# Moving VectorE's division and store of an attention head behind the second maxima of the next heads

## The reference

```python
def softmax_attend(q, k, v):
    s = jnp.einsum('bkgqd,bksd->bkgqs', q, k).astype(F32) * HEAD_DIM ** -0.5
    p = jax.nn.softmax(s, axis=-1).astype(v.dtype)
    return jnp.einsum('bkgqs,bksd->bkgqd', p, v)
```

## Time and profile before

| | |
|---|---|
| median of 3 executions | 6648.83 us (6646.48 to 6653.36) |
| the profiled execution | 6653.24 us |
| its span in the trace | 6651.5 us |
| TensorE busy | 4964.1 us, 75% of the span |
| VectorE busy | 2852.6 us, 43% |
| ScalarE busy | 1478.4 us, 22% |
| mean granted TensorE clock | 0.838 of full speed |

### The profile page before, as it was taken

One profiled execution on the slowest core, in us unless ns is written; L12 is line 12 of the kernel. 1 busy time (PEld: TensorE's weight loads), 2 busy tenths in 40 slices (PEclk: granted clock), 3 DMA queues, 4 the chain that ended last, 5 costly groups with the idle time before them and its releaser, 6 DMA issues. The chain is left out here.

```text
span 6651.5 us, 79229 instructions
## 1 busy us (share of the span) xinstructions
PE 4964.1 (75%) x26926; PEld 4081.8 (61%) x26926; DVE 2852.6 (43%) x3626; ACT 1478.4 (22%) x1933; POOL 1309.9 (20%) x1432
## 2 busy tenths in 40 slices
PE   3996754777667749999975988727777576599995
PEld 2884443666546638888864864516666465477774
DVE  5443465554444352222334224454554444433233
ACT  3113232111121232111213122231111212232221
POOL 0001101111134023223311010102111243143332
PEclk8997887888855879999987998868888655799997
DMA  3441000000000111111112330000000100111112
GB/s 144 155 159 38 28 18 8 0 0 0 8 32 0 34 44 42 38 35 34 32 51 71 119 128 8 28 26 0 0 0 0 40 0 14 57 48 47 44 44 76
DMA packets 59810, 274.70 MB, mean 41 GB/s; under 512 B 6672, under 2 KB 6928, under 8 KB 54544
## 3 DMA queue, kind: packets, MB, share of 16 engines
q1 hardware_dynamic: 43824, 191.23, 8.8%
q10 hardware_dynamic: 15840, 81.53, 3.4%
HBM read 214.80 MB, written 50.07 MB: 40 GB/s over the span
## 5 line engine op out<-in xcount | busy, mean ns | idle before, releaser
L1712 PE MATMUL b<-qp,kr 64*128 64x128 f32 x2560 | 381.5, 448 | 219.5 <-PEq L1702 126.4
L430 PE MATMUL ps<-h_hi,wu_hi 128*128 128x512 f32 (+1 forms) x1760 | 483.5, 372 | 45.2 <-PEq L426 40.7
L2415 DVE SCALAR_TENSOR_TENSOR y<-ps,taps,y 128x1023 f32<-128x1023 f32 (+1 forms) x132 | 134.2, 1016 | 855.3 <-DVEq L2413 848.8
L1712 PEld LDWEIGHTS b<-qp,kr 64*128 64x128 f32 x2560 | 302.4, 315 | 296.9 <-issue 296.9
L430 PE MATMUL ps<-h_hi,wu_raw_rest 128*128 128x512 f32 (+1 forms) x1760 | 481.5, 371 | 0.0
L430 PE MATMUL ps<-h_whole_rest,wu_hi 128*128 128x512 f32 (+1 forms) x1760 | 481.4, 371 | 0.0
L2444 POOL TENSOR_TENSOR wu_raw_rest<-wu_raw,wu_hi 128x1024 fp32r<-128x1024 f32 x88 | 210.8, 2396 | 1041.0 <-POOLq L2443 1041.0
L430 PE MATMUL ps<-h_hi,w_hi 128*128 128x512 f32 x1296 | 326.9, 361 | 83.8 <-PEq L426 83.8
L2436 DVE TENSOR_TENSOR xT<-ps,xT 128x1280 f32<-128x1280 f32 (+1 forms) x176 | 239.1, 1358 | 342.2 <-DVEq L2432 342.2
L430 PEld LDWEIGHTS ps<-h_hi,wu_hi 128*128 128x128 f32 x1760 | 308.1, 189 | 110.9 <-issue 53.1
L1360 POOL TENSOR_TENSOR S<-dec,mix 128x512 f32<-128x512 f32 x40 | 50.6, 1264 | 1631.2 <-POOLq L1359 1631.2
(11 more groups left out here) (271 smaller groups left out, 9838.0 us busy)
## 6 DMA issues: line engine op xcount, KB each, us to landing
wu_raw<-in_w_up_dram SPq DMA_DIRECT2D x88, 512.0 KB, 3.6
rows<-rows ACTq DMA_DIRECT2D x54, 640.0 KB, 4.8
w_raw<-in_w_in_dram SPq DMA_DIRECT2D x54, 512.0 KB, 4.7
ada_w<-in_ada_rest_dram ACTq DMA_DIRECT2D x27, 1024.0 KB, 7.2
wd_raw<-in_w_down_dram SPq DMA_DIRECT2D x44, 512.0 KB, 4.2
raw<-rows SPq DMA_DIRECT2D x24, 640.0 KB, 3.9
ada_w<-in_ada_rest_dram ACTq DMA_DIRECT2D x27, 512.0 KB, 5.1
oT<-rows SPq DMA_DIRECT2D x16, 640.0 KB, 5.8
```

The source lines that it names most:

```text
L430: mm = pe.matmul(ps[:, lo:lo + width], w[a][:, t, :], rhs[b][:, t, lo:lo + width], start=(t == 0 and i == 0), stop=(t == n_k - 1 and i == 2))
L1712: mm = pe.matmul(B[d][2 * ((l + 1) % 2) + h % 2][:, a * P:(a + 1) * P], kr[rows, d, a, :], qp[rows, d, a, :], start=True, stop=True)
L2415: dve.scalar_tensor_tensor(y[:, s, lo + 1:hi], ps[s][:, lo:hi - 1], k.taps[:, s, 0:1], y[:, s, lo + 1:hi], ALU.mult, ALU.add).then_inc(own ...
```

## The change

The place of `output(n - 1)` in VectorE's list is changed. It comes behind unit 1 in windowed attention and for the context heads, and behind unit 2 in global attention. No instruction is added or removed, and the lists of the other engines stay as they are.

```diff
                         if rows_after(n, i):
                             rows(n + 1)
-                        if n and i == 0:
+                        if n and i == (1 if window or n > 7 else 2):
                             output(n - 1)
```

## The result

The kernel after the change takes 6701.62 us (median of 4 executions, 6698.57 to 6703.93) against 6650.12 us before (4 executions). The ratio is 1.0077, with a 95% interval of 1.006 to 1.0095: slower by about 51 us. The profiled execution after took 6698.57 us, with a span of 6696.8 us.

The account below looks back on a forecast made before the run. TensorE's list was taken to set the pace, with one wait per head on VectorE at `scores`. Terms 0 + 26.4 + 6.4 - 4 + 13 = 42 us on 6648.8 gave a median of 6691 us, range 6672 to 6706.

Parts of the forecast that it names:

- Global heads, 0 us: 13 global heads: TensorE's wait for VectorE moves from p2 to p3, nothing gained or lost, within 0.1 us each.
- Windowed heads, 26.4 + 6.4 us: 12 windowed heads: output queued behind the sink wait makes p3 late, 2.64 us in ten heads, 3.21 in two.
- TensorE quicker after a wait, 4 us back: Windowed heads: steps after a long wait run faster, about 0.3 us per head over 12 heads, 4 us back.
- The clock, 13 us: Windowed heads: TensorE's longer wait drops its clock in nearly each of 12 heads, 1.1 us each, 13 us.
- The last heads of layer 2, counted as nothing: Last two windowed heads of layer 2: they make no maxima, so no cost was counted for the moved output.
- the longer windowed stretch: Sign in the profile after: the stretch of 12 windowed heads is 30 to 45 us longer.
- rival 2: Windowed heads: clock falls and stays low, up to 3 us per head; 6714 us, or 6705 or so; chance 0.08.
- That the clock would not fall (6678): Windowed heads: wait grows, but the clock doesn't fall or only inside the wait; 6678 us (6672 to 6683); chance 0.20.
- No change: Windowed heads only exchange one wait for another, as global ones do; 6649 us, within 5; chance 0.06.
- Faster: Global and windowed heads: VectorE's chain fits between p1 and p3, so the wait goes; 6623 us; chance 0.04.

Follow-up runs that it names:

- The run of this part alone: Kernel before with the output moved only in global heads 1 to 7 (behind unit 2): 6650.82 against 6649.54 us, ratio 1.0001.
- the run with the row behind p2: Changed kernel with the next head's row behind p2 in windowed heads, after the output: 6662.38 us against 6651.39 for the kernel before, ratio 1.0017.
- the run with quarters everywhere: Kernel before with latent heads' output cut into four quarters, one behind each maximum, in global and windowed attention: 6674.89 against 6651.39 us, ratio 1.0035.
- the filled wait: Changed kernel plus nine unused TensorE matmuls ahead of p3 in windowed heads: 6686.57 us against 6649.54 for the kernel before, ratio 1.0054.

## Why the prediction was right, and which terms were off

**Global heads, 0 us.** Right. The chain that was worked out, 7.04 us from one reduction to TensorE's next step, ran from p1 instead of p0, and p3 was reduced 12.31 us after p0 where it had been 12.33. (TensorE's matmuls wait at most 0.8 us there in both kernels; the 1.2 us that I gave is the wait of a windowed head.) The run of this part alone shows no difference.

**Windowed heads, 26.4 + 6.4 us.** Right in mechanism and size. 2.64 us per ordinary head were predicted, 2.69 measured; in heads 6 and 7 of layer 1, 3.21 were predicted, and by the same reckoning p3 came 3.09 and 3.25 us late. The wait at the sinks was 1.59 us (1.5 predicted), TensorE's wait 3.84 us. For that wait I had said about 3.3; my own figures, 862.86 less 859.0 to 859.5, give 3.4 to 3.9. That the sinks' wait is what the output is queued behind was tested by putting the output ahead of it: the loss fell from 51 to 18 us.

**TensorE quicker after a wait, 4 us back.** Mis-sized. With the clock held at 1.00 the heads were 15.52 us apart. The neighbouring heads before, 851.50 and the next at 864.38, are 12.88 apart; the difference of 2.64 is the late p3, with nothing given back. The 0.33 us of the earlier trace rows are there in one step; why the head as a whole doesn't keep them was not tested.

**The clock, 13 us.** Right in kind, too small: 17.09 - 15.52 = 1.57 us per head instead of 1.1, some 19 us in 12 heads, all of which have the fall in the trace. I had taken a middle between a fall that lies half inside the wait and one that lies behind it. In the trace the low stretch lies behind the wait whole (3.2 us of work at 0.50), which is the upper bound of 1.5. Head 6 of layer 1, with its 6.3 us at 0.50, lost more: 5.65 us from p0 to p0, of which 3.09 are the late p3.

**The last heads of layer 2, counted as nothing.** That step failed. The timeline of TensorE after shows a wait there for output(5), which now stands behind the last row:

```profile
4391.14 1.13 PE L2102 MATMUL outs<-prob,VO 128*128 128x512 f32 x2 [2.23 <-DVE oT L2216]
```

It is some 2.2 us. I had looked for maxima only, and not for the second thing that waits for the output, the first `values` of the next head. It can also cost clock: at the same wait in the run with the row behind p2 the clock fell, here it stayed at 1.00. The same omission spoiled the run with quarters everywhere.

**Sum.** With the measured terms: 26.9 + 6.4 + 19 + 2.2 = 54.5 us, against 51.5 between the medians. The windowed phases themselves agree: from the first reduction of head 1 to the end of the last product it was 102.6 us in layer 1 and 81.9 in layer 2, and is 133.9 and 105.6, 55.0 us more in all. The profiled executions differ by only 45.3 us (6698.57 - 6653.24) because the unchanged work between the two layers' attention took 3076.0 us before and 3065.5 after; with the same windowed attention and the global one left alone it took 3072.4. The medians may hold such differences of unchanged stages too.

So the number came out better than the sum behind it. I had put my bounds at 32 to 52 us and the longer windowed stretch at 30 to 45. The measured terms, 54.5 us, lie above both, since all three errors (nothing given back, more for the clock, the wait in the last heads) go the same way. The total is inside the stated range because that range was stretched over the lower part of rival 2.

**Rivals.** That the clock would not fall (6678) is out by the rows of 0.50 and by the filled wait. That it would stay low (6714) is out: in an ordinary head it is back at 1.00 before the next, and only one head of 12 has a low stretch of 6.3 us. No change holds for the global heads and for them alone. Faster needed VectorE's chain to fit between TensorE's steps; whole it doesn't, cut it does.

## What to carry to other kernels

A piece of work on a helping engine that is longer than the distance between two steps of the leading engine cost a wait at every place where it was tried here; moving it past one step moves the wait, and moving it also past an instruction that waits for a third engine adds that wait to it. What removed the wait was cutting the piece to fit the gaps, as far as its own deadline allows; so list every consumer of the moved work, the one that waits for its buffer too. And a wait of the matmul engine has a second price behind it, in clock, which can be more than half of the first.

## What was not expected of the hardware

A wait of 2.1 to 2.3 us left the clock at 1.00 in nine heads of 12 and took it to 0.50 in three, while waits of 3.7 to 4.1 us were followed by 0.50 in all 12 heads of the changed kernel. A wait of 2.23 us at the same instruction was followed by 1.00 in the changed kernel and by 0.50 with the row behind p2. Nine matmuls whose result nobody uses made the kernel 14 us faster (51 to 37). A division of 64x512 takes 3.36 us, of 64x256 1.74 and of 64x128 0.96, so cutting costs about 0.12 to 0.16 us for each further piece.
